# Ten unit-matrix products behind each inner layer of the filter network, the modulation's first chunk between the last taps, one rounding operation less

## What is computed

```
def hyena_filters(L, w1, b1, w2, b2, w3, freq):
    ...
    hdn = jnp.sin(f[0] * (z @ w1.astype(F32) + b1.astype(F32)))
    hdn = jnp.sin(f[1] * (hdn @ w2.astype(F32) + b2.astype(F32)))
    filt = (hdn @ w3.astype(F32)).reshape(L, HYENA_ORDER, 2, B_WIDTH)
    ...
    return filt * jnp.exp(-t * deltas)[:, None, None, :]

def modulation(cond, w, b):
    m = jax.nn.silu(cond) @ w + b
    return jnp.split(m[..., None, :], 6, axis=-1)
```

## Time and profile before

| | us |
|---|---|
| three runs | 4229.21, 4231.39, 4233.12 (median 4231.39) |
| profiled execution | 4230.91 |
| its span in the profile | 4229.1 |
| TensorE busy | 4042.5 |
| VectorE busy | 1308.5 |
| ScalarE busy | 683.1 |
| GpSimd busy | 387.0 |

### The profile page before, as it was taken

The page is one execution under the profiler, slowest core; times in us unless marked ns, Lnnn a source line. Parts: engine busy times, 40 slices in busy tenths (PEclk is TensorE's granted clock), DMA queues, the critical chain, the costliest instruction groups (busy, mean ns, idle before and its releaser), DMA issues. The chain is left out here.

```text
span 4229.1 us, 60812 instructions
## 1 busy us (share of the span) xinstructions
PE 4042.5 (96%) x26396; PEld 3549.3 (84%) x26396; DVE 1308.5 (31%) x3032; ACT 683.1 (16%) x1679; POOL 387.0 (9%) x361
## 2 busy tenths in 40 slices
PE   8999999989799999999998999999969999999996
PEld 4777786574499999999997888886459999999995
DVE  6434453485602121200004625334640000000003
ACT  0122221103210101101114111111410101111111
POOL 0000000252400000000003000000330000000002
PEclk9999999999899999999999999999979999999998
DMA  8410001224578888777763010103247777777775
GB/s 327 167 32 28 18 18 59 71 82 150 193 289 299 316 293 312 297 275 273 280 247 125 31 35 16 48 18 123 93 164 279 273 282 273 277 283 268 284 279 209
DMA packets 146853, 781.16 MB, mean 185 GB/s; under 512 B 14809, under 2 KB 51321, under 8 KB 100507
## 3 DMA queue, kind: packets, MB, share of 16 engines
q1 hardware_dynamic: 137370, 743.71, 47.2%
q0 software_dynamic: 9216, 33.56, 3.8%
HBM read 721.03 MB, written 56.20 MB: 184 GB/s over the span
## 5 line engine op out<-in xcount | busy, mean ns | idle before, releaser
L2334 PE MATMUL PS<-arena 128*128 128x144 f32 x11264 | 1441.6, 287 | 1.5 <-ACT arena L764 1.5
L2334 PEld LDWEIGHTS PS<-arena 128*128 128x128 f32 x11264 | 1406.8, 190 | 2.5 <-ACT arena L764 2.3
L2315 PE MATMUL PS<-arena 128*128 128x144 f32 x5632 | 742.6, 286 | 0.0
L2315 PEld LDWEIGHTS PS<-arena 128*128 128x128 f32 x5632 | 711.4, 190 | 1.6 <-DVE arena L2441 1.6
L2441 DVE TENSOR_TENSOR arena<-PS,arena 128x144 f32<-128x144 f32 x352 | 108.4, 308 | 1892.7 <-ACT arena L2406 1892.7
L2406 ACT ACTIVATE arena<-PS 128x144 f32<-128x144 f32 x352 | 102.5, 291 | 1698.4 <-PE PS L2334 1698.4
L1893 PE MATMUL PS<-arena 128*128 128x512 f32 x576 | 259.8, 600 | 2.3 <-PEq L3218 1.8
L2798 PE MATMUL PS<-arena 128*128 128x256 f32 x1152 | 253.4, 381 | 1.7 <-ACT arena L3014 1.7
L2845 PE MATMUL PS<-arena 128*128 128x256 f32 x1152 | 254.4, 379 | 0.0
L2798 PEld LDWEIGHTS PS<-arena 128*128 128x128 f32 x1152 | 218.5, 191 | 31.9 <-issue 2.8
L2272 POOL DMA_INDIRECT expert_sum<-arena x32 | 52.7, 1646 | 2067.2 <-DVE arena L2389 2067.2
(11 more groups left out here) (376 smaller groups left out, 3433.1 us busy)
## 6 DMA issues: line engine op xcount, KB each, us to landing
arena<-expert_panels SPq DMA_DIRECT2D x352, 1536.0 KB, 6.7
arena<-ada_w SPq DMA_DIRECT2D x6, 4096.0 KB, 16.3
arena<-ada_w SPq DMA_DIRECT2D x12, 2048.0 KB, 11.7
arena<-odd_w_in SPq DMA_DIRECT2D x16, 1024.0 KB, 6.0
arena<-hgrn_w SPq DMA_DIRECT2D x20, 512.0 KB, 4.0
arena<-filter_spectra SPq DMA_DIRECT2D x36, 256.0 KB, 2.8
mid_rows<-arena SPq DMA_DIRECT2D x18, 512.0 KB, 2.9
filter_spectra<-arena SPq DMA_DIRECT2D x16, 512.0 KB, 4.2
```

The costliest lines, as they stand in the source:

```text
L2315: m = pe.matmul(PS[:, m_ // 3, m_ % 3 * SLOTS:m_ % 3 * SLOTS + SLOTS], s.w2[n % RING][:, m_ * P:(m_ + 1) * P], s.hid[:, f, :], start=f == ...
L2334: m = pe.matmul(PS[:, 6 + n % 2, q * 256:q * 256 + SLOTS], s.w13[n % RING][:, q, k, :], s.xs[e % 2][:, k, :], start=k == 0, stop=k == KD - 1)
```

## The change

Four edits, all in the first stage. (1) `spare_products` puts ten products of the unit matrix with itself (128x128, into bank 5, which nobody reads) behind each of the two inner layers; TensorE waits for their end by its own semaphore. (2) `ada_w` chunk 0 is loaded ahead of all four spectra. (3) Chunk 0 of the modulation is cut up: steps 0 and 1 behind tap 3, then 2 and 3 behind tap 4, 4 and 5 behind tap 5, 6 behind tap 6, 7 behind tap 7. The wait for its load now stands behind tap 3. (4) The multiplication and the addition of `BIG` become one operation on VectorE.

```
             def row_steps(s, pe, q, steps):
                 for k in steps:
...
                 for dst, src in ((s.dec, I["decay_lat"]), (s.drow, I["hyena_bias"][0:1]),
                                  (s.decc, I["decay_ctx"]), (s.specc, I["spec_ctx"])):
                     sp.dma_start(dst, src).then_inc(s.dl, 16)
+                m.load(sp, 0)
                 for kt in (0, 2, 1, 3):
-                    if kt == 1:
-                        m.load(sp, 0)
                     sp.dma_start(s.spec[:, kt], I["spec_lat"][kt]).then_inc(s.spl[kt], 16)
...
+            def spare_products(s, pe, n, count):
+
+                for i in range(count):
+                    m = pe.matmul(PS[:, 5, 0:P], ident, ident, start=True, stop=True)
+                m.then_inc(s.spare, 1)
+                pe.wait_ge(s.spare, n + 1)
...
                     if layer == 0:
                         m.pe_cond(pe)
+                    s.spare_products(pe, layer, 10)
                 pe.wait_ge(s.hok, 3)
                 pe.wait_ge(s.w3l, 32)
                 for j in range(8):
                     s.pe_taps(pe, 0, j)
-                m.rows(pe, 0)
+                    if j == 3:
+                        pe.wait_ge(m.cond, 2)
+                        pe.wait_ge(m.wl[0], 16)
+                    if j >= 3:
+                        mm = m.row_steps(pe, 0, ((0, 1), (2, 3), (4, 5), (6,), (7,))[j - 3])
+                mm.then_inc(m.full, 1)
...
-                    ch.link(dve.tensor_scalar(s.rnd, s.arg, 1.0 / (2 * math.pi), None, ALU.mult))
-                    ch.link(dve.tensor_scalar(s.rnd, s.rnd, BIG, None, ALU.add))
+                    ch.link(dve.tensor_scalar(s.rnd, s.arg, 1.0 / (2 * math.pi), BIG, ALU.mult, ALU.add))
                     ch.link(dve.tensor_scalar(s.rnd, s.rnd, -BIG, None, ALU.add))
```

More of the change, by code:

```diff
@@ L276, in rows, with row_steps @@
                 pe.wait_ge(s.wl[q % 2], 16 * (q // 2 + 1))
-                for k in range(KD):
+                s.row_steps(pe, q, range(KD)).then_inc(s.full, 1)
+            def row_steps(s, pe, q, steps):
+                for k in steps:
                     for j in range(4):
@@ L280, in rows @@
                                       s.W[q % 2][:, k, j * 256:(j + 1) * 256], start=k == 0, stop=k == KD - 1)
-                m.then_inc(s.full, 1)
+                return m
             def add_bias(s, dve, q):
@@ L488, in __init__ @@
                 s.st, s.stc = [sm(f"stored{b}") for b in range(2)], sm("ctx_stored")
+                s.spare = sm("spare_products")
             def sync(s, sp):
```

## The result

| | before | after |
|---|---|---|
| median, 20 executions each | 4230.12 us | 4236.78 us |
| lowest and highest | 4227.80, 4233.12 | 4233.16, 4239.02 |
| profiled execution | 4230.91 | 4236.86 |
| its span | 4229.1 | 4235.0 |

The changed kernel is **slower by 6.66 us**, ratio 1.0015 with a 95% interval of 1.0008 to 1.0021. The forecast was 4232.2, its range ended at 4235.0: the prediction was wrong. The first stage, about which all of it was, did nearly what was forecast; the rest of the loss came hundreds and thousands of microseconds later. The measured 4236.8 lies close to rival C's 4237.2, but that is chance: C's cause, a load that lands no earlier, did not occur.

What follows compares the result with a forecast made beforehand. TensorE, busy 96% of the span, was taken as the bound, with the first stage's chain ending at VectorE's L712; its start moving from 45.00 to 46.3 gave 4230.9 + 1.3 = 4232.2 us, range 4224.5 to 4235.0.

Steps and rivals of the forecast that it cites:

- rival C: First stage: ada_w's load lands no earlier, TensorE waits behind tap 3 until 33.6; 6.3 us lost, 4237.2; chance 0.05.
- Layer 1 and the operation less: Before the taps: one rounding operation less saves 1.06 us, layer 1 falls to about 1.4; taps start at 21.4 or 20.2.
- The load: Load queue: ada_w moved ahead of the spectra lands at 28.5 instead of 33.6, and TensorE waits for it behind tap 3.
- The sum of the alternation: TensorE from 28.6 at 1.2 GHz: chunk steps 6.8, taps 8.2, changes 0.6, L599 2.1, so L712 starts at 46.3.
- The clock: TensorE from 28.6: 1.2 GHz expected through the alternation of chunk and taps, rising only near 46 to 48.
- rivals A and B: First stage: A, mixture raises the clock, 3.5 to 5.3 us gained, 0.33; B, clock stays high, 7.1 us gained, 0.08.
- whatever the twenty products did: TensorE at 28.6: 1.2 GHz expected regardless of the added products, because sparse taps and a wait come before.
- The mark: End of the first stage: VectorE's L712, the first operation on the context's filter, starts at 46.3 instead of 45.00.
- What moves it moves the rest: Behind VectorE's L712: any shift of its start reaches the end, so 1.3 us there is 1.3 us in all.
- Cost nothing: Ten products behind each inner layer: 2.2 us at 2.4 GHz or 4.4 at 1.2 GHz, hidden in TensorE's waits.
- The cap on the gain: First stage: ada_w's landing at 28.5 limits any gain to near 7 us.
- The range: Whole kernel: 4224.5 to 4235.0 us, taking in the forecast with the runs' spread and rival A.

Runs made afterwards that it cites:

- fused: Kernel before with only the two VectorE rounding operations made into one; 4228.48 us, ratio 0.9997.
- whole: Changed kernel with the chunk's 32 products in one piece behind tap 7; 4232.60 us, ratio 1.0005.
- afterpad: Changed kernel with 44 tiny products more in TensorE's idle time, 256 products and weight loads added in all; 4234.64 us, ratio 1.0009.
- noprod: Changed kernel without the twenty unit-matrix products; 4231.96 us, ratio 1.0005.
- warm: Changed kernel with 31 more full-size unit products behind layer 1 and taps 1 to 3, 204 entries added in all; 4231.37 us, ratio 1.0002.
- late3: Kernel before with three more VectorE operations in layer 1, a delay ahead of the taps; 4231.33 us, ratio 1.0004.
- best: Changed kernel with 23 more full-size products, 21 tiny ones and the bias loaded right behind ada_w's first chunk, 256 entries added; 4229.19 us, ratio 0.9996.
- warmpad: As warm, with 13 tiny products behind tap 1, so 256 entries added instead of 204; 4228.57 us, ratio 0.9997.
- pad81: Kernel before with ten tiny products behind each inner layer and a wait for them, in TensorE's idle time; 4234.74 us, ratio 1.0010.
- the two pairs of kernels: whole (4232.60 us) and the same with 44 tiny products more (4228.38); pad81 (4234.74) and pad256 (4229.23).
- pad256: Kernel before with 32 tiny products behind each inner layer, in idle time, 256 entries added; 4229.23 us, ratio 0.9997.

## Why the prediction was wrong, by its own steps

**Layer 1 and the operation less: right.** The taps start at 20.45 (forecast 20.2), layer 1 takes 1.29 us (1.4). The operation alone was worth 1.06 us plus what the clock made of it (fused). That the first ten products raised the clock in time was in part luck: it rose at 11.1 in after and at 13.7 in whole, and in afterpad layer 1 was still slow behind the same ten. A slip without effect: sixteen records in 1.95 us are 0.12 us each and not 0.11, so ten products cost 2.4 us at the full clock (measured 2.50) and 4.6 at the low one (4.64 in whole, 4.63 in afterpad). They ended by 13.1, still inside the cover.

**The load: right.** It landed at 28.7 (28.5), and TensorE waited for it behind tap 3, so the chunk started at 28.80, 0.5 us ahead of noprod's, and no more was left of the front's 2 us.

**The sum of the alternation: right.** From the first chunk product to the mark it was 17.7 us by forecast and 17.76 measured (28.80 to 46.56). A tap was put at 2.05 and took 2.07; the chunk's steps were put at 0.85 and took 0.96 to 1.08 with the change of weights, which was counted apart.

**The clock: right in after, with less behind it than was said.** It rose at 11.1, fell at 21.3 and stayed low until 48.6; rivals A and B did not come. The fall came 0.9 us into the taps, behind 3.01 us in which TensorE had nothing to do (17.44 to 20.45). The wait for the load came 6.5 us later and did not cause it. In A's favour nothing happened in 15 us of alternation. But warm shows that the products can raise the clock and the alternation keeps it, if there are enough of them and no wait: the prediction's "whatever the twenty products did" holds for twenty. And late3 and fused show that the rise is less fixed than the sum took it: 40.0 to 42.7 in three kernels with the same row of taps and chunk. In best and warmpad, which came to the chunk at the low clock, the rise followed on some 5 us of full-row products without a tap between them.

**The mark: this is the step that failed.** "What moves it moves the rest" made 1.3 us at the mark into 1.3 us at the end. Measured were 1.56 at the mark and 5.95 at the end. The term behind it is the twenty products' "Cost nothing", for which only the cover in the first stage was weighed. There they cost nothing and gave 0.5 us (noprod). Their 81 entries in TensorE's list cost 4.75 us in pad81 with none of the change's other edits, and taking them out of after left +0.1 at the end and 1.55 in the median (noprod). The prediction had all entries of the list before it and counted only their time.

How much of this is explained: the step at 2725 (1.7 us) is shown, by the packet in the store's stretch and the stores' 2.9 to 3.0 us in all three kernels with 81 entries, and by the lack of this step in every kernel with another number. The longer wait at 958 goes the same way. For the steps at 2933 and 3076 (1.1 and 0.9 us) the two pairs of kernels speak, and warm (204 entries) has them; but afterpad, with 256, has both as well, and warmpad, with 256, the second. What the fourteen traces do show is where the clock's fall stands against the work. Near 2925 after's work stood 3.9 us later than before's, but its clock fell only 2.5 us later, so 1.4 us earlier against the work, and it stayed low for 6.8 us instead of 3.4. So it is in all of them: in the five with 6.8 us (after, whole, pad81, afterpad, warm) the fall came 0.1 to 1.8 us earlier against the work than in before, in the other eight at most 0.03 us earlier and up to 0.6 later. Near 3070 it came 1.7 to 3.1 us earlier in the six with 23.9 us and within 0.2 us of before's in the rest. In the three kernels with 81 entries the late stores held the work up by 1.0 to 1.2 us (what was left of their step at 2922) without the clock's fall moving along, and that is one way from the list to the low clock; afterpad and warm show that there are others. So the list's length is a likely cause of these two steps, not a shown one. The step at 622 (1.6 us) is in after and best (1.5) and in no other kernel, 81 entries or not. It stays open whether it comes back in every execution; the median of after, 6.66 above before, is no smaller than its profiled 5.95, but pad81, without this step, was 2 us slower in the median than in its trace too, so that proves little.

**The cap on the gain: too high.** "The landing at 28.5 caps the gain near 7 us" overlooked the bias. With it the cap was 45.00 - 41.81 = 3.2 us, as warm measured. It did not matter for after.

**The range.** It held the first stage's cases and the spread of three runs (3.9 us), and nothing for what happens beyond the stage. The only case above 4235 was C, at 0.05. The profiled execution of before, from which the sum was made, also stood 0.8 us above the median of twenty (4230.91, 4230.12), so the miss in the change itself is 5.4 us and not 4.6.

## What to carry to other kernels

An instruction has a place in its engine's list as well as a duration. Here 81 entries in idle time moved the later instruction packets by 84 records against the work (pad81), and 2.7 ms further on VectorE's wait for two small stores was 4.30 us where it is 2.27 in before. So count what an edit adds, and before blaming or praising the edit, time it once more padded to the distance of the packets, here 256 entries (afterpad shows that not all of the loss need come back). Where a local gain doesn't show at the end, match the two traces from the last instruction backwards: the difference of the start times names the places in a few steps. And before work is cut up to start it earlier, look whether the pieces run at the clock that the whole has, and which other load is wanted at the new time.

## What the runs showed of the hardware

The queue "instruction" had one packet of 16 KB for every 255.3 to 256.0 TensorE records (all fourteen traces). Where such a packet came 1.1 to 1.8 us behind the issue of two 128 KB stores near 2725, these took 2.9 to 3.0 us to landing (after, whole, pad81) instead of 1.8 (before, pad256); where one came at 954 to 960, a wait for a load took 6.3 to 6.5 us instead of 5.3 to 5.7. 81 entries that did next to nothing cost 4.75 us (pad81), 256 of them nothing that could be measured (pad256, 0.86 us below before).

Half-row taps in a dense row did not raise the clock (11 us in before), nor did their alternation with full-row products in nearly 16 us, when it began at the low clock (after: share 0.50; noprod: 1.93 us for 16 chunk records, as in after); begun at the full clock, the same alternation kept it (warm: share 1.00 from 29.74 through the end of L623 at 39.25).

The clock's rise came 2.4 us after the chunk's start in late3, 3.2 us in fused and 4.8 us in before, with the same products in the same order ahead of it. Why is open.
